# Eight size classes for routed experts instead of five (160, 224 and 288 tokens added)

## What is computed

```python
def moe_swiglu(h, w_router, b_router, w1, w3, w2):
    logits = (h @ w_router).astype(jnp.float32) + b_router.astype(jnp.float32)
    top_v, top_i = lax.top_k(logits, TOP_K)
    gates = jax.nn.softmax(top_v, axis=-1)
    combine = jnp.sum(jax.nn.one_hot(top_i, N_EXPERTS, dtype=jnp.float32) * gates[..., None], axis=-2)
...
    for e in range(N_EXPERTS):
        out = out + combine[..., e:e + 1] * swiglu(h, w1[e], w3[e], w2[e])
    return out
```

## Time and profile before

| | us |
|---|---|
| median of the runs | 2049.78 (2048.74 to 2050.16) |
| span of the profiled execution | 2050.2 |
| PE busy | 1776.2 (87%) |
| DVE busy | 1332.1 (65%) |
| ACT busy | 811.6 (40%) |
| from the first matmul of e0 to the last of e7 | 1300.2 to 2001 |
| router, tables and first gather ahead of them | about 1222 to 1300 |

### The profile page before, as it was taken

The page is one execution under the profiler, slowest core; times in us unless marked ns, Lnnn a source line. Parts: engine busy times, 40 slices in busy tenths (PEclk is TensorE's granted clock), DMA queues, the critical chain, the costliest instruction groups (busy, mean ns, idle before and its releaser), DMA issues.

```text
span 2050.2 us, 32403 instructions
## 1 busy us (share of the span) xinstructions
PE 1776.2 (87%) x11246; PEld 1594.4 (78%) x11247; DVE 1332.1 (65%) x2391; ACT 811.6 (40%) x1300; POOL 280.5 (14%) x280
## 2 busy tenths in 40 slices
PE   4898799999999999996477976798979799997992
PEld 1596399999999999992233764798968789997992
DVE  1587756568878784478885538344857678874445
ACT  1435424322122232322466333333744577753331
POOL 1000100000000000049910001002010122101012
PEclk9999899999999999995599998899989899998995
DMA  8333323446754351520000003336865799966334
GB/s 239 123 124 125 116 69 93 136 130 196 239 165 144 111 152 57 144 77 20 3 1 0 22 27 113 95 104 191 273 202 178 222 323 313 323 212 192 117 104 165
DMA packets 312644, 289.12 MB, mean 141 GB/s; under 512 B 20874, under 2 KB 301674, under 8 KB 312468
## 3 DMA queue, kind: packets, MB, share of 16 engines
q1 hardware_dynamic: 298292, 249.28, 39.3%
q0 software_dynamic: 12272, 34.50, 5.3%
q10 hardware_dynamic: 1904, 3.13, 0.5%
HBM read 263.38 MB, written 23.47 MB: 140 GB/s over the span
## 4 chain that ended last, share of the span: by engine, by line
PE 74%; DVE 11%; issue 7%; ACT 4%; DMA 2%; ACTq 1%; DVEq 0%; POOL 0%; POOLq 0%
PE ps L1264 19%; PE ps L1265 18%; PE ps L1266 18%; PE ps L1269 6%; PE ps L1270 3%; PE ps L1376 2%; DVE vp L2343 2%; PE ps L1307 1%; PE ps L1326 1%; DVE lo L1977 1%; ACT hi L770 1%; PE ps L1586 1%; PE ps L1701 1%; DVE hot L2579 1%; DMA y_rows<-rows_y 1%
## 5 line engine op out<-in xcount | busy, mean ns | idle before, releaser
L770 ACT ACTIVATE hi<-raw 128x1024 fp32r<-128x1024 f32 (+3 forms) x442 | 394.7, 919 | 559.6 <-PE ps L1266 474.3
L1977 DVE TENSOR_TENSOR lo<-raw,hi 128x1024 fp32r<-128x1024 f32 (+3 forms) x442 | 458.2, 1057 | 242.1 <-ACT hi L770 238.2
L1264 PE MATMUL ps<-h_wide,hi 128*128 128x320 f32 (+1 forms) x1728 | 542.0, 314 | 23.3 <-issue 17.1
L1265 PE MATMUL ps<-h_wide,hi 128*128 128x320 f32 (+1 forms) x1728 | 537.4, 311 | 0.0
L1266 PE MATMUL ps<-h_wide,lo 128*128 128x320 f32 (+1 forms) x1728 | 537.2, 311 | 0.0
L1264 PEld LDWEIGHTS ps<-h_wide,hi 128*128 128x128 f32 x1728 | 327.6, 190 | 26.3 <-issue 23.9
L1265 PEld LDWEIGHTS ps<-h_wide,hi 128*128 128x128 f32 x1728 | 327.4, 189 | 0.4 <-issue 0.2
L1266 PEld LDWEIGHTS ps<-h_wide,lo 128*128 128x128 f32 x1728 | 327.5, 190 | 0.0
L1264 PE MATMUL ps<-g_both,hi 128*128 128x320 f32 x528 | 166.7, 316 | 2.6 <-DVE g_both L2284 2.6
L1265 PE MATMUL ps<-g_both,hi 128*128 128x320 f32 x528 | 163.6, 310 | 0.0
L1266 PE MATMUL ps<-g_both,lo 128*128 128x320 f32 x528 | 163.6, 310 | 0.0
(11 more groups left out here) (381 smaller groups left out, 2825.8 us busy)
## 6 DMA issues: line engine op xcount, KB each, us to landing
raw<-in_moe_w_dram SPq DMA_DIRECT2D x160, 512.0 KB, 5.2
raw<-in_w_mod_dram SPq DMA_DIRECT2D x96, 512.0 KB, 4.5
raw<-in_moe_w_dram SPq DMA_DIRECT2D x96, 384.0 KB, 3.6
raw<-in_ff_w_dram SPq DMA_DIRECT2D x40, 512.0 KB, 4.7
raw<-in_moe_w_dram SPq DMA_DIRECT2D x64, 256.0 KB, 3.4
y_rows<-zeros POOLq DMA_DIRECT2D x22, 512.0 KB, 4.4
raw<-in_ev_w_in_dram SPq DMA_DIRECT2D x12, 512.0 KB, 5.8
raw<-in_ff_w_dram SPq DMA_DIRECT2D x16, 384.0 KB, 4.2
```

What stands on the lines that cost most here:

```text
L770: act.activation(hi[c % 2][:, parts[h]], raw[slot][:, parts[h]], ACT.Copy).then_inc(hi_done, 1)
L1264: pe.matmul(out, w_hi, v_hi, start=first, stop=False, skip_group_check=True)
L1265: pe.matmul(out, w_hi, v_lo, start=False, stop=False, skip_group_check=True)
L1977: dve.tensor_tensor(lo[c % 2][:, parts[h]], raw[ring_of(c) % 4][:, parts[h]], hi[c % 2][:, parts[h]].bitcast(F32), ALU.subtract).then_inc( ...
```

## The change

`SIZES` and `TILES` grow to eight entries. `by_size` becomes a function that halves the list of classes and calls itself, so that there are eight bodies in the loop and eight behind it, with three compares on each path. `tiles_of`, `gather_first` and `gather_more` ask by the number of tiles (`holds`) instead of by fixed class numbers. DVE's table code does seven compares and one reduction where it did four compares and three additions, and skips the steps in which the number of tiles doesn't grow.

```diff
-SIZES = ((128, 1), (192, 1), (256, 1), (TH, 1), (TH, 2))
-TILES = (1, 2, 2, 3, TT)
+SIZES = ((128, 1), (160, 1), (192, 1), (224, 1), (256, 1), (288, 1), (TH, 1), (TH, 2))
+TILES = (1, 2, 2, 2, 2, 3, 3, TT)
...
+        def by_size(eng, size, body, kinds=SIZES, below=0):
+            if len(kinds) == 1:
+                body(*kinds[0])
+                return
+            cut = (len(kinds) + 1) // 2
+            with eng.If(size < below + cut):
+                by_size(eng, size, body, kinds[:cut], below)
             with eng.Else():
+                by_size(eng, size, body, kinds[cut:], below + cut)
+
+        def holds(size, count):
+            return size > sum(n < count for n in TILES) - 1
...
-            link(dve.tensor_tensor(cnt[:, 0, :], cnt[:, 1, :], cnt[:, 2, :], ALU.add))
-            for i in range(2, len(SIZES) - 1):
-                link(dve.tensor_tensor(cnt[:, 0, :], cnt[:, 0, :], cnt[:, 1 + i, :], ALU.add))
+            link(dve.tensor_reduce(cnt[:, 0, :], cnt[:, 1:len(SIZES), :].rearrange("p s e -> p e s"), AX_X, ALU.add))
...
             for i in range(len(SIZES) - 1):
+                if TILES[i + 1] == TILES[i]:
+                    continue
```

More of the change, by code:

```diff
@@ L105 @@
     0, 8, 24, 28, 36, 44, 52, 56, 60, 64, 68, 76, 84, 92, 93)
-SIZES = ((128, 1), (192, 1), (256, 1), (TH, 1), (TH, 2))
-TILES = (1, 2, 2, 3, TT)
-Y_TILES = NE * TILES[0] + 3 * (TILES[4] - TILES[0]) + (TILES[3] - TILES[0])
+SIZES = ((128, 1), (160, 1), (192, 1), (224, 1), (256, 1), (288, 1), (TH, 1), (TH, 2))
+TILES = (1, 2, 2, 2, 2, 3, 3, TT)
+Y_TILES = NE * TILES[0] + 3 * (TILES[-1] - TILES[0]) + (TILES[-2] - TILES[0])
 IDENT, BEFORE, SWAP = range(3)
@@ L465, in gather_tiles @@
             return [(g, min(P, total - P * g)) for g in range((total + P - 1) // P)]
[L467 to L476, removed]
+        def by_size(eng, size, body, kinds=SIZES, below=0):
[5 more added lines that the diff above has]
+                by_size(eng, size, body, kinds[:cut], below)
             with eng.Else():
[L478 to L481, removed]
+                by_size(eng, size, body, kinds[cut:], below + cut)
+        def holds(size, count):
+            return size > sum(n < count for n in TILES) - 1
         def tiles_of(eng, size, tile):
             tile(0)
-            with eng.If(size > 0):
+            with eng.If(holds(size, 2)):
                 tile(1)
-            with eng.If(size > 2):
+            with eng.If(holds(size, 3)):
                 tile(2)
-            with eng.If(size > 3):
+            with eng.If(holds(size, TT)):
                 tile(3)
@@ L1710, in gather_first @@
                 turn_rows(0)
-                with pe.If(size > 0):
+                with pe.If(holds(size, 2)):
                     turn_rows(1)
@@ L1718, in later @@
                     turn_rows(g)
-                with pe.If(size > 2):
+                with pe.If(holds(size, 3)):
                     later(2)
-                with pe.If(size > 3):
+                with pe.If(holds(size, TT)):
                     later(3)
```

## The result

| | us |
|---|---|
| before, median of 12 runs | 2050.44 (2048.74 to 2054.87) |
| changed, median of 12 runs | 2055.84 (2051.54 to 2059.45) |
| ratio | 1.0023, 95% interval 1.0014 to 1.0032 |
| span of the profiled execution, before and changed | 2050.2 and 2056.5 |

The change makes the kernel slower by 0.23%, 4.7 us. The forecast was 2048.2, 0.1% faster, so the change went the other way; 2055.84 lies inside the range of 2039 to 2060 and on the side of the second rival, the dear jumps.

The account below looks back on a forecast made before the run. PE was taken as the bound in e0, e2 and e6, with code fetch in the starts. Gains of 20.8 us against 19.2 of costs gave 2048.6, less 0.4 for the median: 2048.2 us, 8-in-10 range 2039 to 2060.

Parts of the forecast that it names:

- dear jumps: Rival at e0, e6 and e7 starts: each target drags its neighbour's fetch; cost 31 us, total 2060, chance 0.18.
- What bounds the kernel: PE, busy 87% of the span, bounds e0, e2 and e6; long gaps ahead of experts are code fetch.
- Narrower matmuls: e0 at 288 columns saves 11.7 us, e2 at 448+224 saves 8.2, half-clock first stretches 0.6 more.
- The tables of DVE: DVE's chain of additions, which PE waits for, gets shorter: gain 0.3 us.
- e0, one more jump, +3.8: Start of e0: two jumps instead of one cost 3.8 us more (2.8 to 7).
- e2, +0.5: Start of e2: still two jumps, first target now farther; 0.5 us more (0 to 3.5).
- one of them is only exchanged: Gap ahead of e2: of its three code packets, more than one far jump needs, one is merely exchanged; +0.5 us.
- e6, +8.6: Start of e6: its body no longer follows the one just run; two-place gap, 8.6 us more (4 to 12.2).
- Half clock behind e6, +2.5: After e6's new gap PE runs at the lower clock, losing 2.5 us (1.5 to 3).
- e7, one more jump, +3.8: Start of e7: two jumps instead of one cost 3.8 us more (2.8 to 7).
- DVE and ACT hidden: DVE and ACT take the same longer paths, but their 3 or 4 us more stay hidden behind PE.
- The rule weighed against the rows: Skill's two-block fetch window would mean nothing new at e6; rejected since three starts wait only about half a us.

Follow-up runs that it names:

- x20: Changed kernel with four extra TensorE waits (two instructions) ahead of its expert loop; 2045.2 us, 0.9975 of before.
- x18: Before with four extra TensorE waits (two instructions) ahead of its expert loop; 2047.3 us, 0.9977 of before.
- x5: Changed kernel with all comparisons at the head of the loop, so one jump reaches each body; 0.9926 of before.
- x3: Changed kernel without its class of 160 columns, which no expert takes; 2032.8 us, 0.9910 of before.
- x6: Changed kernel with 32 extra TensorE waits (16 instructions) ahead of its expert loop; 0.9984 of before.
- x14: Seven classes (the change without 160) with all comparisons at the head of the loop; 0.9861 of before.
- x2: Changed kernel with its eight bodies, but e0's and e2's compute before's 320 and 256 columns; 1.0126 of before.
- x9: Before's five bodies and tree with widths 128, 192, 224, 288 and twice 320, class 320 dropped by mistake; 2191.4 us, 1.0690 of before.
- x4: Before with an unused sixth body of 160 columns, plus the changed kernel's DVE table code; 1.0203 of before.
- x13: x5 cut to six classes (128, 192, 224, 288, 320, twice 320), all comparisons at the loop's head; 1.0067 of before.
- x7: x4 with 128 extra DVE waits ahead of DVE's loop, moving its code by 64 instructions; 1.0045 of before.
- x17: x13 with four extra DVE waits (two instructions) ahead of DVE's loop; 2018.3 us, 0.9839 of before.
- x16: Before's five classes with all comparisons at the head of the loop, nothing else changed; 0.9998 of before.

## Why the prediction was wrong, by its own steps

The gains came in as forecast (21.0 us in the two bodies against 20.5); the costs didn't. Of the 19.2 us for jumps and half clock the profile shows 27.3, and with that the sign turned. All four gaps were priced too low, e6's by most (8.6 against 11.8), and the sum had no term for where in the program a jump lands.

- **What bounds the kernel**: right. PE's columns in e0 and e2 and PE's gaps are the whole difference. The reading of the long gaps as the fetch of code is now shown, since waits that only move code change them by 6 us and take one packet of code out of them.
- **Narrower matmuls**: right. 12.0 forecast for e0, 10.9 measured; 8.5 for e2, 10.1 measured. Inside e2's body of the changed kernel a pair of 448+224 columns takes 0.316 us, from these two, eleven pairs apart; forecast 0.320, and 264 pairs make 1.0 us of the 1.6 more.

```profile
1537.08 0.37 PE L1268 MATMUL ps<-h_wide,hi 128*128 128x448 f32 x1
...
1540.56 0.37 PE L1268 MATMUL ps<-h_wide,hi 128*128 128x448 f32 x1
```

- **The tables of DVE**: 0.3 forecast and measured.
- **e0, one more jump, +3.8**: mis-sized, 5.8 (the upper bound was 7; x20 against x18 gives 4.6). x5 and x3, which reach this body by one jump, give the 6 us back; x6 and x20, which only move code, don't. So it is the jump.
- **e2, +0.5, "one of them is only exchanged"**: near in size (+2.1), wrong in content. Before, e2's 12.69 us were one jump to code not in place and a body that began at a bad position, 14610; x18 moves it by two instructions and e2 starts after 6.92. In the changed kernel its body begins elsewhere, and a second such jump has come in: 14.18 us in x20. So the jump is worth 7.3 us and the position 5.8, and the forecast's "exchanged" was two effects that nearly cancelled.
- **e6, +8.6**: this is the step that failed most, 11.8. I noticed that e6's new place was within an instruction of e2's old one, with its 12.69 us, and then set that row aside for the average of two others, on the ground that some of its packets were for the loop's tail. The row was right, to 0.4 us (12.35 less 0.53 is 11.8, against the upper bound of 12.2). Half of it is the position: 6.51 us in x20.
- **Half clock behind e6, +2.5**: right, 2.1.
- **e7, one more jump, +3.8**: mis-sized and, as a cause, wrong. 5.5 were added, but in x20 the same two jumps take 9.33 us, as one did before. What moved it was again code moved by two instructions, though no body of e7's begins at the place that the other gaps point to. The packets on q8 in the gap follow it here too: the changed kernel has five from 1870.3 to 1885.3 us, x20 three from 1862.6 to 1872 us, as before has.

```profile
q8 instruction: 5, 0.08, 3.1%
```

```profile
q8 instruction: 3, 0.05, 3.1%
```

In the other kernels two go with 6.5 us (x5), three with 9.3 to 11.4, four with 12.1 (x14) and five with 14.5 to 15.2 (x2, x3, x9). What sets the number stays open: x3 and x9 reach e7 by two jumps, x14 and x5 by one, and by jumps alone they follow no rule that I could find.
- **DVE and ACT hidden**: right for the changed kernel, and by luck. Its DVE loop begins at 2096; in x4 and x13, at 2094, the same engine costs 32 and 47 us (against x7 and x17). I had looked at how much longer DVE's path got, and not at whether its code would still be held.
- **The rule weighed against the rows**: e6 waits 12.35 us where 0.53 stood, so code that had stayed in place before was lost. The Trainium skill ("Runtime: NRT & Kernel Launch", section "Instruction fetch mechanics") has only two blocks near the program counter at hand, by which nothing new would have come at e6; the trace disagrees once more. That a branch out of what is at hand forces a fetch, as it says, fits: every gap of 6.5 us and more ahead of a body's first matmul has packets on q8.
- **The rivals**: dear jumps came nearest by its total (2060; measured 2055.8), and e6's upper bound of 12.2 with it; its mechanism, the neighbour's fetch, was not tested. With both codes moved by two instructions, x20 against x18, the ratios are 0.9975 and 0.9977: no difference. That is the forecast's result, but on other terms: 4.6 us at e0, 7.3 at e2, 6.0 at e6, -0.6 at e7 and 2.1 of half clock (taken over from the changed kernel), 19.4 against 21 of columns.

## What to carry to other kernels

A body chosen at run time costs twice: for its columns, and for the jump to it, 5 to 7 us on TensorE here for each further target that isn't in place. Put all comparisons at the head, the bodies that follow each other side by side, and leave out classes that the data don't use; with DVE's loop moved by two instructions that turned +4.7 us into -33. Which classes those are is known here from the token counts of one input; no run has another routing. Before a change that moves code is judged, move the code of both versions by two instructions and measure again: so moved, the 5 us by which this change lost were gone.

## What the runs showed of the hardware that was not expected

- A jump's price steps by 5.8 us when its target moves by two instructions: 12.69 us and three packets in before, 6.92 and two in x18, which differ in nothing else. Across kernels that differ in more, the step lies between 14611 (12.55 us, x16) and 14612 (7.22, x13). I take it for a border between two 16 KB blocks of code, which must then come one after the other; the missing packet bears that out, though no row shows where a block begins.
- On VectorE two instructions decide over waits of 12 us at each of the small experts e4 and e5 and of more at e2 and e6: x13, with the loop's head at 2094, has them, and x17, at 2096, has none at e4, e5 and e6 and 8.3 us at e2. At 2095 (x3 and x14, with other classes) e4 and e5 have none either. Why there is a step at just this place is argued from positions alone.
- Code that has run can stay in place past a change of body: in x17 q8 has no packet from 1558 to 1576 us, around e3's start, and PE waits there 2.21 and 1.26 us for data, where 10.17 stood for code. Why it stayed there and not in before, no run isolates. The queues, then the matmul that turns e2's last results and e3's first:

```profile
q1 hardware_dynamic: 4895, 4.86, 84.7%
q0 software_dynamic: 341, 0.62, 9.1%
q14 instruction: 1, 0.01, 0.1%
```

```profile
1573.55 0.65 PE L1882 MATMUL ps<-mats,tmp 128*128 128x128 f32 x4 [2.21 <-DVE tmp L2743]
1575.45 0.55 PE L1262 MATMUL ps<-hi,h_wide 128*128 128x256 f32 x1 [1.26 <-DVE lo L1975]
```
